# A decoder trunk on one core: the norm update's squares, gates and adds divided anew among ScalarE, VectorE and GpSimd

## The chip, the core and the metric

The kernel runs on one core of a Trainium2 chip. The metric is the device time of one execution in microseconds; the time of a kernel is the median of several executions. Five engines work side by side and meet through semaphores: TensorE (PE) multiplies matrices into PSUM, VectorE (DVE), ScalarE (ACT) and GpSimd (POOL) work elementwise, and SyncE (SP) issues most of the DMAs.

## The reference

One inference step of a trunk of four layers, D = 1024, on a prompt of 512 tokens and 8 sample sequences of one token each. Layers 0 and 3 mix tokens with a short convolution ("sconv"), layer 1 with RWKV-7, layer 2 with gated linear attention ("gla"); each is followed by a convolutional FFN ("up", "down"). Every half layer has the same frame:

```python
def rmsnorm(x, g, eps=RMS_EPS):
    xf = x.astype(jnp.float32)
    y = xf * lax.rsqrt(jnp.mean(xf * xf, axis=-1, keepdims=True) + eps)
    return (y * g.astype(jnp.float32)).astype(x.dtype)

# in trunk(), for each layer l; mod comes from the conditioning vector c
u = rmsnorm(h, norm_g[l, 0]) * (1 + sc_m) + sh_m
out = mixer(u)
h = h + gt_m * rmsnorm(out, norm_g[l, 1])
u = rmsnorm(h, norm_g[l, 2]) * (1 + sc_f) + sh_f
out = conv_ffn(u)
h = h + gt_f * rmsnorm(out, norm_g[l, 3])
```

The change is about `h = h + gate * rmsnorm(out)` and the norm of h behind it. There are eight such updates. The first follows the "out" stage of layer 0, the second the "down" stage of layer 0 (the rwkv layer comes next), and so on to the eighth, which follows "down" of layer 3 and leads to the output.

## The kernel before

All activations are held transposed: 128 channels on the partitions, tokens along the free dimension, so that h is 8 tiles of 128x520 (512 prompt tokens and 8 sample tokens) in SBUF. Weights come in blocks of 128 output channels. SyncE loads a block into one of two w_raw slots (line 523); ScalarE rounds it to w_hi (line 1037, `high`); GpSimd subtracts to get w_lo (line 814, `low`, or in four pieces in line 821, `low_parts`); TensorE runs x_hi w_hi, x_lo w_hi and x_hi w_lo (lines 1722 and 1730). SyncE may load a slot anew once the w_lo of the block in it is made. Its DMAs are issued in the order of the program, each behind its own wait, so one that waits holds all behind it.

A `plan` lists the stages in order: "pre" (the norm ahead of a half layer), the mixer's stages, "out" (output projection), "post" (the update), "pre", "up", "down", "post". Every engine walks through the plan and emits its part; nothing is reordered.

In "out" and "down" a tile of 128 output channels ends in two PSUM banks. ScalarE copies it to the SBUF slab `proj` (lines 1106 and 1107). VectorE squares it (line 3202) and adds the square to csb (lines 3217, 3225); the last tile's square is made by ScalarE straight from PSUM (`square_last`, lines 1100 and 1101).

In "post", TensorE sums the squares over the channels with ones (line 1784), ScalarE takes the root (line 1063), VectorE the reciprocal (line 2641), and TensorE spreads it over the partitions into PSUM (lines 1826 and 1828). Then, tile by tile, VectorE multiplies `proj` by it (line 2695) and does h = h + gate x proj with the gate as a scalar per partition (line 2751). Line 2739 to 2743 do the same for the sample columns. In the "pre" behind it ScalarE squares every new tile of h (line 1072) and TensorE sums it (line 1784), with two buffers between them; root, reciprocal and spreading follow once more; VectorE multiplies h by the result (line 2695), ScalarE applies scale and shift twice (lines 1137 and 1139, or 1128 and 1130 ahead of rwkv), and VectorE makes the low part. With the first tile of that the next weight matmuls begin.

Each half layer's modulation is made ahead of time by small matmuls of the conditioning vector with ada_w (line 1683). For the halves 2 to 7 part of them stands in the norm stages: 8 columns' worth in "post", and in the sums of "pre" one group behind each of the fourth to seventh sum. For those, SyncE loads six buffers (`ada_ahead`, line 547) anew after their first use (`load_again`). In the rwkv layer's first stage ("rproj"), SyncE's order is: the first weights, the rank weights w_raw from a1 and w1, the last rank weight g1, which waits for the w_lo of the block before it, and then `load_again`. GpSimd there multiplies the rank weights by a factor (line 865) and makes their low parts (line 875).

At the end TensorE transposes h back: first the sample columns of all eight tiles (line 2570), which are ready before any prompt tile and are released by the first count of h_ready, then tile by tile (line 2579); ScalarE and VectorE copy the result to y_rows, and SyncE stores it.

## Time and profile before

| | |
|---|---|
| Time, median of 3 executions | 2992.96 us (2991.05 to 2993.82) |
| The profiled execution | 2992.34 us, of which the span from first to last instruction 2990.5 us |
| Busy: PE, weight load, DVE, ACT, POOL | 95%, 91%, 51%, 36%, 44% of the span |
| Mean granted TensorE clock | 0.975 of full speed |
| DMA | 332.59 MB, 111 GB/s in the mean |

Durations in this document come from that one profiled execution. A row of the timeline has the start in us from the span's start, the time in us, the engine, the line, the operation, output<-inputs, how many instructions were merged (xN), and in brackets the idle time ahead of it and what ended it. "PEld" is TensorE's weight load, "SPq" SyncE issuing a DMA. A matmul in fp32 appears as two records. TensorE runs at 2.4 GHz or, where the throttle grants half, at 1.2 GHz.

### The profile page before, as it was taken

To read this page: it belongs to the slowest core of one execution; us is meant where nothing else is said; L and a number is where in the kernel's file an instruction comes from. 1 tells how busy PE (TensorE), PEld (TensorE's weight loads), DVE (VectorE), ACT (ScalarE), POOL (GpSimd) and SP (SyncE) were. 2 spreads that over 40 slices of the span, in tenths; PEclk is the share of its full clock that TensorE was granted. 3 is DMA by queue.
4 is the path that set the end of the run, shared out by engine and by line. 5 is a ranking of instruction groups with operands and counts; after the bars stand their busy time and mean duration, and the time that the engine had idled before them with its cause. 6 is when DMAs were issued, how large, how long until landed. Compare 5 with 4: busy or idle time off the path is not lost. (4 is left out here: it accounts for less than half of the span.)

```text
span 2990.5 us, 71312 instructions
## 1 busy us (share of the span) xinstructions
PE 2845.7 (95%) x29353; PEld 2711.8 (91%) x29353; DVE 1535.0 (51%) x2080; ACT 1062.6 (36%) x2047; POOL 1314.5 (44%) x957
## 2 busy tenths in 40 slices
PE   6999999998998999899999899999999999899998
PEld 5998999997988986899998799889999899799998
DVE  3445766117446885676603342476650444577612
ACT  3224333225455652433323543343332422433322
POOL 3443544442434563354443273434444344355443
PEclk8999999998999999999999999999999999899999
DMA  7544333444411004333344323533334543233332
GB/s 268 166 149 171 92 91 91 157 128 135 121 51 31 4 12 136 123 91 91 104 157 154 112 64 113 171 120 91 91 116 149 172 125 86 64 91 91 90 93 86
DMA packets 462286, 332.59 MB, mean 111 GB/s; under 512 B 16567, under 2 KB 432261, under 8 KB 461791
## 3 DMA queue, kind: packets, MB, share of 16 engines
q1 hardware_dynamic: 460148, 325.80, 35.2%
q10 hardware_dynamic: 1930, 3.68, 0.5%
q8 instruction: 172, 2.82, 0.4%
q14 instruction: 36, 0.29, 0.0%
HBM read 319.66 MB, written 10.20 MB: 110 GB/s over the span
## 5 line engine op out<-in xcount | busy, mean ns | idle before, releaser
L814 POOL TENSOR_TENSOR w_lo<-w_raw,w_hi 128x1024 fp32r<-128x1024 f32 x394 | 1005.0, 2551 | 1095.3 <-ACT w_hi L1037 1074.7
L1722 PE MATMUL banks<-u_hi,w_hi 128*128 128x260 f32 x4016 | 812.6, 283 | 18.9 <-ACT w_hi L1037 18.9
L1722 PE MATMUL banks<-u_lo,w_hi 128*128 128x260 f32 x4016 | 812.1, 283 | 0.0
L1722 PEld LDWEIGHTS banks<-u_hi,w_hi 128*128 128x128 f32 x4016 | 620.5, 189 | 29.4 <-issue 24.3
L1722 PEld LDWEIGHTS banks<-u_lo,w_hi 128*128 128x128 f32 x4016 | 621.6, 189 | 0.0
L1037 ACT ACTIVATE w_hi<-w_raw 128x1024 fp32r<-128x1024 f32 x402 | 424.6, 1057 | 463.9 <-PE banks L1730 296.7
L1730 PE MATMUL banks<-u_hi,w_lo 128*128 128x260 f32 x4016 | 520.7, 282 | 0.0
L1730 PEld LDWEIGHTS banks<-u_hi,w_lo 128*128 128x128 f32 x4016 | 497.0, 188 | 0.0
L1722 PE MATMUL banks<-hid_hi,w_hi 128*128 128x260 f32 x1664 | 336.4, 283 | 0.5 <-DVE hid_lo L2683 0.5
L1722 PE MATMUL banks<-hid_lo,w_hi 128*128 128x260 f32 x1664 | 335.1, 283 | 0.0
L3202 DVE TENSOR_TENSOR csb<-proj 128x520 f32 (+1 forms) x42 | 30.2, 719 | 470.2 <-ACT proj L1107 470.2
L2683 DVE TENSOR_TENSOR hid_lo<-prod,hid_hi 128x520 f32 x104 | 262.0, 2520 | 12.8
L1722 PEld LDWEIGHTS banks<-hid_hi,w_hi 128*128 128x128 f32 x1664 | 256.7, 188 | 5.7 <-issue 3.7
L1722 PEld LDWEIGHTS banks<-hid_lo,w_hi 128*128 128x128 f32 x1664 | 256.1, 188 | 0.0
L2667 DVE SCALAR_TENSOR_TENSOR conv<-gate,vecs,conv 128x536 f32<-128x536 f32 x104 | 246.9, 2374 | 15.1 <-DVE conv L2665 0.8
L1730 PE MATMUL banks<-hid_hi,w_lo 128*128 128x260 f32 x1664 | 217.0, 282 | 0.0
L1730 PEld LDWEIGHTS banks<-hid_hi,w_lo 128*128 128x128 f32 x1664 | 206.4, 188 | 0.0
L832 POOL TENSOR_TENSOR tails<-gate,ones 128x2 f32 (+1 forms) x104 | 29.2, 281 | 328.9 <-ACT gate L1595 328.9
L1602 ACT ACTIVATE conv<-conv,vecs 128x536 f32<-128x536 f32 x88 | 65.5, 744 | 288.2 <-DVE conv L2667 288.2
L1593 ACT ACTIVATE gate<-banks 128x260 f32<-128x260 f32 x88 | 34.1, 387 | 356.4 <-PE banks L1730 355.7
L2664 DVE TENSOR_SCALAR conv<-gate,vecs 128x536 f32<-128x536 f32 x104 | 57.9, 556 | 177.0 <-ACT gate L1595 173.0
L2665 DVE SCALAR_TENSOR_TENSOR conv<-gate,vecs,conv 128x536 f32<-128x536 f32 x104 | 113.8, 1095 | 15.2 <-DVE conv L2664 1.6
(471 smaller groups left out, 3840.0 us busy)
## 6 DMA issues: line engine op xcount, KB each, us to landing
w_raw<-in_ffn_w_up_dram SPq DMA_DIRECT2D x176, 512.0 KB, 3.7
ada_raw<-in_ada_w_dram SPq DMA_DIRECT2D x96, 512.0 KB, 4.7
w_raw<-in_ffn_w_down_dram SPq DMA_DIRECT2D x64, 448.0 KB, 3.7
w_raw<-in_sconv_w_in_dram SPq DMA_DIRECT2D x48, 512.0 KB, 5.0
ada_ahead<-in_ada_w_dram SPq DMA_DIRECT2D x36, 512.0 KB, 7.2
ada_ahead_down<-in_ada_w_dram SPq DMA_DIRECT2D x36, 512.0 KB, 5.9
w_raw<-in_ffn_w_down_dram SPq DMA_DIRECT2D x32, 512.0 KB, 4.0
ada_pro<-in_ada_w_dram SPq DMA_DIRECT2D x6, 2048.0 KB, 21.5
```

The lines of the kernel that those rows point to most:

```text
L814: pool.tensor_tensor(w_lo[:, s, :, :], w_raw[:, s, :, :], w_hi[:, s, :, :].bitcast(F32), ALU.subtract).then_inc(lo_done, 1)
L832: pool.tensor_tensor(to[:, 0:2], gate[:, e, TP:TP + 2], ones[:, 0:2], ALU.mult).then_inc(pool_step, 1)
L1037: act.activation(w_hi[:, s, :, :], w_raw[:, s, :, :], ACT.Copy).then_inc(hi_done, 1)
L1593: act.activation(gate[:, e, 2:2 + HALF], tile_ps[0][0][:, 0:HALF], ACT.Copy)
L1602: act.activation(conv[:, e, 0:CWD], conv[:, e, 0:CWD], ACT.Silu, bias=vec("ffn_conv_b", l * FT + m)).then_inc(silu_done, 1)
L1722: pe.matmul(tile_ps[slot][half][:, 0:HALF], w_hi[:, s, k, :], x[:, k0 + k, half * HALF:(half + 1) * HALF], start=start and k == 0 and i == ...
L1730: mm = pe.matmul(tile_ps[slot][half][:, 0:HALF], w_lo[:, s, k, :], xh[:, k0 + k, half * HALF:(half + 1) * HALF], start=False, stop=stop an ...
L2664: link(dve.tensor_scalar(conv[:, e, 0:CWD], gate[:, e, 0:CWD], w[0], None, ALU.mult))
L2665: link(dve.scalar_tensor_tensor(conv[:, e, 0:CWD], gate[:, e, 1:1 + CWD], w[1], conv[:, e, 0:CWD], ALU.mult, ALU.add))
L2667: dve.scalar_tensor_tensor(conv[:, e, 0:CWD], gate[:, e, 2:2 + CWD], w[2], conv[:, e, 0:CWD], ALU.mult, ALU.add).then_inc(conv_done, 1)
L2683: dve.tensor_tensor(lo, prod[:, e, :], hi.bitcast(F32), ALU.subtract).then_inc(hid_ready, 1)
L3202: return dve.tensor_tensor(csb[:, 1, :], o, o, ALU.mult)
```

## The change

In "out" and "down" ScalarE squares every tile straight from PSUM (`square_tile`): tile 0 into csb's first half, every other tile into the second, and VectorE only adds. The copy out of PSUM becomes `evacuate_gated`: three instructions, of which the two for the prompt tokens apply the gate as the activation's scale. In "post" VectorE multiplies two tiles at a time by the spread root and then adds tiles 3 to 7 to h; GpSimd adds tiles 0 to 2. There are two semaphores in place of one (`early_ready` for tiles 0 to 2, `h_ready` for 3 to 7), and GpSimd, ahead of its next w_lo, waits until all adds of the update are done. ScalarE's loops over "out" are written out. Some semaphores of the states of layers 1 and 2 are merged to make room for the new ones; the counts that are waited for stand for the same events.

```diff
+EARLY = 3
+LATE = KT - EARLY
+SUMMED = KT - 2
...
+                if p["kind"] == "post":
+                    for k in range(EARLY):
+                        pool.wait_ge(scaled_pair, KT // 2 * p["post"] + k // 2 + 1)
+                        pool.tensor_tensor(h[:, k, 0:TP], h[:, k, 0:TP], p["proj"][:, k, 0:TP], ALU.add)\
+                            .then_inc(early_ready, 1)
+                    if n0 < NBLK:
+                        pool.wait_ge(h_ready, LATE * (p["post"] + 2))
...
-                    act.wait_ge(h_ready, hs + k + 1)
+                    if k < EARLY:
+                        act.wait_ge(early_ready, EARLY * hs + k + 1)
+                    else:
+                        act.wait_ge(h_ready, LATE * hs + k - EARLY + 1)
...
-            def square_last(s, n, index):
-
-                act.wait_ge(sum_ready, index + 1)
+            def square_tile(s, n, index, m):
+
+                dst = csb[:, min(m, 1), :]
+                if m >= 2:
+                    act.wait_ge(sum_ready, SUMMED * index + m - 1)
                 act.wait_ge(block_done, n + 3)
-                act.activation(csb[:, 1, 0:HALF], tile_ps[s][0][:, 0:HALF], ACT.Square)
-                act.activation(csb[:, 1, HALF:T], tile_ps[s][1][:, 0:HALF], ACT.Square).then_inc(last_squared, 1)
+                act.activation(dst[:, 0:HALF], tile_ps[s][0][:, 0:HALF], ACT.Square)
+                act.activation(dst[:, HALF:T], tile_ps[s][1][:, 0:HALF], ACT.Square).then_inc(tile_squared, 1)
+
+            def evacuate_gated(s, n, mod, m, dst):
+
+                gain = mod[:, 2 * KT + m, 0:1]
+                act.wait_ge(block_done, n + 3)
+                act.activation(dst[:, TP:T], tile_ps[s][1][:, TP - HALF:HALF], ACT.Copy)
+                act.activation(dst[:, 0:HALF], tile_ps[s][0][:, 0:HALF], ACT.Copy, scale=gain)
+                return act.activation(dst[:, HALF:TP], tile_ps[s][1][:, 0:TP - HALF], ACT.Copy, scale=gain)
...
-            h_first = KT * 2 * depth
-            pe.wait_ge(h_ready, h_first + 1)
+            posts = 2 * depth
+            pe.wait_ge(h_ready, LATE * posts + 1)
             for k in range(KT):
                 mm = pe.transpose(bank[Y_RIGHT[k // 4]][0:NS, (k % 4) * P:(k % 4 + 1) * P], h[:, k, TP:T], ident[:, :])
             mm.then_inc(y_turned, 1)
             for k in range(KT):
-                pe.wait_ge(h_ready, h_first + k + 1)
+                if k < EARLY:
+                    pe.wait_ge(early_ready, EARLY * posts + k + 1)
+                else:
+                    pe.wait_ge(h_ready, LATE * posts + k - EARLY + 1)
...
-                    for k in range(KT + 1):
-                        if k < KT:
-                            step[0] += 1
-                            times_rstd(proj_x[:, k, :], proj_x[:, k, :]).then_inc(dve_step, 1)
-                        if k:
-                            dve.wait_ge(dve_step, base[0] + step[0] - (k < KT))
-                            dve.scalar_tensor_tensor(h[:, k - 1, 0:TP], proj_x[:, k - 1, 0:TP],
-                                                     mod[:, 2 * KT + k - 1, 0:1], h[:, k - 1, 0:TP], ALU.mult,
-                                                     ALU.add).then_inc(h_ready, 1)
+                    pairs = KT // 2
+                    for k in range(0, KT, 2):
+                        two = proj_x[:, k:k + 2, 0:TP]
+                        dve.tensor_tensor(two, two, rstd_ps[0].unsqueeze(1).to_broadcast([P, 2, TP]), ALU.mult)\
+                           .then_inc(scaled_pair, 1)
+                    for k in range(EARLY, KT):
+                        dve.wait_ge(scaled_pair, pairs * p["post"] + k // 2 + 1)
+                        dve.tensor_tensor(h[:, k, 0:TP], h[:, k, 0:TP], proj_x[:, k, 0:TP], ALU.add).then_inc(h_ready, 1)
...
+                    def add_square(m):
+
+                        dve.wait_ge(tile_squared, KT * index + m + 1)
+                        if m > 1:
+                            dve.wait_ge(sum_ready, SUMMED * index + m - 1)
+                        dve.tensor_tensor(csb[:, 0, :], csb[:, 0, :], csb[:, 1, :], ALU.add).then_inc(sum_ready, 1)
```

The order of instructions on GpSimd at the second update, between the "down" stage of layer 0 and the rank weights of the rwkv layer (L865 and its successor L876 scale them); before:

```order
L814 TENSOR_TENSOR w_lo<-w_raw,w_hi 128x1024 [waits hi_done]
L1010 REGISTER_ALU
L1010 COMPARE_AND_BRANCH
L821 TENSOR_TENSOR w_lo<-w_raw,w_hi 128x256 [waits hi_done]
L821 TENSOR_TENSOR w_lo<-w_raw,w_hi 128x256 x3
L865 TENSOR_TENSOR w_raw<-w_raw,vecs 128x8x64 [waits w_loaded0]
L865 TENSOR_TENSOR w_raw<-w_raw,vecs 128x8x64
L865 TENSOR_TENSOR w_raw<-w_raw,vecs 128x1024 [waits w_loaded1]
```

And the same place on GpSimd in the changed kernel:

```order
L818 TENSOR_TENSOR w_lo<-w_raw,w_hi 128x1024 [waits hi_done]
L1021 REGISTER_ALU
L1021 COMPARE_AND_BRANCH
L846 TENSOR_TENSOR h<-h,proj 128x512 [waits scaled_pair] x3
L825 TENSOR_TENSOR w_lo<-w_raw,w_hi 128x256 [waits hi_done,h_ready]
L825 TENSOR_TENSOR w_lo<-w_raw,w_hi 128x256 x3
L876 TENSOR_TENSOR w_raw<-w_raw,vecs 128x8x64 [waits w_loaded0]
L876 TENSOR_TENSOR w_raw<-w_raw,vecs 128x8x64
L876 TENSOR_TENSOR w_raw<-w_raw,vecs 128x1024 [waits w_loaded1]
```

The three adds and the wait on h_ready stand ahead of the w_lo pieces now. SyncE's order at the same place, in the changed kernel (L527 loads a weight block, L551 a buffer of modulation columns); before it has the same rows as L523 and L547:

```order
L527 DMA w_raw<-in_rwkv_w_dram 128x8x64 [waits lo_done,pack_loaded]
L527 DMA w_raw<-in_rwkv_g_dram 128x8x128 [waits lo_done]
L551 DMA ada_ahead_down_190<-in_ada_w_dram 128x1024 [waits ada_used]
L551 DMA ada_ahead_down_191<-in_ada_w_dram 128x1024 [waits ada_used]
L551 DMA ada_ahead_down_192<-in_ada_w_dram 128x1024 [waits ada_used]
```

Nothing moved on SyncE; the load of the rwkv_g weights waits on lo_done, which the w_lo pieces count. The order on TensorE at the output, in the changed kernel (L2587 turns the sample columns, L2599 the tiles):

```order
L2587 MATMUL banks<-ident,h 8x128 [waits h_ready]
L2587 MATMUL banks<-ident,h 8x128 x7
L2599 MATMUL banks<-ident,h 128x128 [waits early_ready]
L2599 MATMUL banks<-ident,h 128x128 x3
L2599 MATMUL banks<-ident,h 128x128 [waits early_ready]
```

Before, all of these wait on h_ready, whose first count stood for tile 0; now its first count of an update stands for tile 3.

## Rows read from the trace of the kernel before

**Rows 1.** Groups by line, ScalarE: busy us, mean ns | idle before us, what ended it

```profile
L1106 ACT ACTIVATE proj<-banks 128x260 f32<-128x260 f32 (+1 forms) x48 | 18.6, 388 | 170.5 <-PE banks L1730 170.5
```

**Rows 2.** Timeline, first update: start us, us, engine, line, operation [idle before <-releaser]

```profile
260.73 1.29 DVE L2695 TENSOR_TENSOR proj<-proj,banks 128x512 f32<-128x512 f32 x2 [0.19 <-PE banks L1828]
...
264.45 0.74 DVE L2751 SCALAR_TENSOR_TENSOR h<-proj,mod_m,h 128x512 f32<-128x512 f32 x1
...
265.92 0.68 PE L1784 MATMUL banks<-csb,ones 128*32 128x136 f32 x8 [0.82 <-ACT csb L1072]
...
267.53 0.68 PE L1784 MATMUL banks<-csb,ones 128*32 128x136 f32 x8
...
269.49 1.41 DVE L2751 SCALAR_TENSOR_TENSOR h<-proj,mod_m,h 128x512 f32<-128x512 f32 x2
...
272.63 0.41 PE L1784 MATMUL banks<-csb,ones 128*32 128x136 f32 x8
```

**Rows 3.** Timeline, third update

```profile
1218.77 1.28 DVE L2695 TENSOR_TENSOR proj_b<-proj_b,banks 128x512 f32<-128x512 f32 x2 [0.19 <-PE banks L1828]
...
1229.00 0.44 PE L1784 MATMUL banks<-csb,ones 128*32 128x136 f32 x8
...
1229.69 0.41 PE L1784 MATMUL banks<-csb,ones 128*32 128x136 f32 x8
```

**Rows 4.** Groups by line, nearest to the new ones; the last: ns min/median/max, first, last start

```profile
L2673 DVE TENSOR_TENSOR prod<-conv,banks 128x260 f32<-128x260 f32 x104 | 44.2, 425 | 89.8 <-ACT conv L1602 79.6 <-PE banks L1730 10.0
...
L2695 DVE TENSOR_TENSOR proj<-proj,banks 128x512 f32<-128x512 f32 x48 | 32.1, 678 | 3.0 <-PE banks L1828 2.9
...
L1595 ACT ACTIVATE gate<-banks 128x8 f32<-128x8 f32 x88 | 16.5, 187 | 0.0
...
L926 POOL TENSOR_TENSOR g_in<-g_in,g_o 128x512 f32<-128x512 f32 x8 | 10.2, 1298 | 3.1 <-ACT g_o L1396 3.1
...
L3225 DVE TENSOR_TENSOR csb<-csb x42: 699/700/2785, 217.6 to 2939.4; 128x520 f32<-128x520 f32 x42
```

**Rows 5.** GpSimd's pieces in the first update; VectorE's small add in all (ns min/median/max)

```profile
259.05 2.79 POOL L821 TENSOR_TENSOR w_lo<-w_raw,w_hi 128x256 fp32r<-128x256 f32 x4 [4.04 <-ACT w_hi L1037]
...
L2743 DVE TENSOR_TENSOR h<-h,s x8: 224/614/745, 259.9 to 2973.0; 128x64 f32<-128x64 f32 x8
```

**Rows 6.** Timeline, second update, and how long the six L547 loads took to land

```profile
671.91 2.77 POOL L821 TENSOR_TENSOR w_lo<-w_raw,w_hi 128x256 fp32r<-128x256 f32 x4
...
674.51 1.28 DVE L2695 TENSOR_TENSOR proj<-proj,banks 128x512 f32<-128x512 f32 x2 [0.43 <-PE banks L1828]
...
675.04 0.58 SPq L523 DMA_DIRECT2D w_raw<-in_rwkv_g_dram  x1
...
675.67 3.50 SPq L547 DMA_DIRECT2D ada_ahead_down<-in_ada_w_dram  x6
...
681.60 0.61 PE L1683 MATMUL banks<-ada_ahead_down,cT 128*32 128x256 f32 x8
...
687.57 0.68 PE L1784 MATMUL banks<-csb,ones 128*32 128x136 f32 x8
...
DMA to landing us min/median/max: 5.5/7.1/9.0
```

**Rows 7.** Timeline, seventh update

```profile
2579.20 1.34 PE L1784 MATMUL banks<-csb,ones 128*32 128x136 f32 x16 [0.58 <-ACT csb L1072]
```

**Rows 8.** Timeline, last update and the transposes of the output

```profile
2974.75 1.29 DVE L2695 TENSOR_TENSOR proj<-proj,banks 128x512 f32<-128x512 f32 x2 [1.50 <-PE banks L1828]
...
2976.76 1.87 PE L2570 MATMUL banks<-ident,h 128*8 128x128 f32 x8 [2.11 <-DVE h L2751]
...
2978.42 3.62 PE L2579 MATMUL banks<-ident,h 128*128 128x128 f32 x16
...
2982.66 1.07 PE L2579 MATMUL banks<-ident,h 128*128 128x128 f32 x8 [0.63 <-ACT y_rows L1641]
...
2984.32 1.32 PE L2579 MATMUL banks<-ident,h 128*128 128x128 f32 x8 [0.58 <-DVE h L2751]
```

More of the change, by code:

```diff
@@ L1114, in _ @@
                     if i:
-                        statistics(i, KT * p["post"], p["half"])
+                        statistics(i, p["post"], p["half"])
                         if p["full"]:
@@ L2613, in _ @@
             dve.wait_ge(x_copied, X0 + KT)
-            for k in range(KT):
-                dve.sem_inc(h_ready, 1)
+            dve.sem_inc(early_ready, EARLY)
+            dve.sem_inc(h_ready, LATE)
             def modulation(l, half, mod):
```

96 lines of the change are left out of this document (38 added, 58 removed).

## The prediction

> **What bounds the kernel now.** I read the page first: TensorE is busy nearly throughout, so time is won or lost only where TensorE stands still or works at its lower clock. The waits, taken by engine, say where the change's own code touches that. In the "out" and "down" stages ScalarE is the one that waits: 170.5 us ahead of 48 copies out of PSUM, 3.6 us each, always for TensorE [rows 1]. Work moved between VectorE and ScalarE there stands beside matmuls. What is left are the eight norm updates, one behind every "out" and "down", where the weight matmuls stop. I read them in the timeline, one by one.
>
> In the first one [rows 2] VectorE's first product with the root starts at 260.73, then product and gated add alternate, a tile every 1.26 us; the third tile of h is started at 264.45 and the last two end at 270.90, 10.2 us after the first product. ScalarE squares each tile and TensorE sums it. TensorE's third sum starts at 265.92, its fourth at 267.53, and from there it does not stop: between the sums it runs the next modulation's columns, 1.3 us a tile, and the eighth sum starts at 272.63, so that it ends 1.0 us later than the last square would allow (270.90, 0.7 for the square and 0.4 for the sum make 272.0; it is 273.0). So here TensorE bounds the end, not VectorE. In those microseconds TensorE is at 1.2 GHz: its 8-matmul sum takes 0.68 us where others take 0.41. In the third update the clock falls later and comes back sooner, and the eighth sum ends 11.3 us after the first product, against 12.3 in the first update [rows 2, 3]; 11.3 is what VectorE's own chain allows. Six of the eight updates have those columns between the sums, two (the last layer's) have not.
>
> **The change part by part.**
>
> *Squares and gates on ScalarE in "out" and "down".* Per tile two squares (0.39 us, as the copies of that shape [rows 1]) and one short copy (0.19 us) [rows 4] come in; VectorE loses a square and keeps the add. 56 of 64 tiles lie beside matmuls and are covered by the 3.6 us that ScalarE waits [rows 1]: nothing. If that cover were gone it would be 56 x 0.97 = 54 us; what is queued behind is the next block's w_hi copy, then GpSimd's w_lo, and both are ready microseconds before their block. At the last tile of a stage the short copy stands ahead of the root: between 0 and its 0.19 us, and the scale operand may add as much; I take 0.1 per update and count it in what follows.
>
> *Products on two tiles.* 128x512 takes 678 ns, 128x260 425 ns [rows 4]: 1.0 ns for an element and 0.16 fixed. A pair is 1.19 us; four follow each other in 4.6 us. Bounds: two old products each (1.29 x 4 = 5.2) and 4 x 1.07.
>
> *Three adds on GpSimd.* A 128x512 add of it takes 1.30 us [rows 4]. The first product pair ends at 1.2, so tiles 0, 1, 2 of h come at 2.5, 3.8 and 5.1 us after the first product. Before, the third came at 264.45 + 0.74 - 260.73 = 4.5. The third tile is 0.6 us later, 0.7 with the short copy.
>
> *Five adds on VectorE.* 0.70 us each [rows 4], start to start 0.62. Products end at 4.6, but VectorE's small add of two SBUF operands took 0.22 us at best and 0.61 in the middle of eight, in updates in which GpSimd's w_lo pieces run beside it [rows 5]; so the first add waits for GpSimd's third, to 5.1. The eighth tile is then there at 5.1 + 0.7 + 4 x 0.62 = 8.3, against 10.2: 1.8 us earlier with the 0.1.
> The Trainium skill (SBUF — State Buffer, Who interferes with whom) states the same as an exclusive lock between the two engines, and its page Perfetto Trace Analysis (Optimizing Scalar/DVE Operations) warns that offloading between these two might not help. Taken for all three adds, that is a rival below. The row beside it: two products, whose second operand is in PSUM, took 1.29 us together while GpSimd was in its four w_lo pieces [rows 2, 5], so products don't wait.
>
> *Five updates with columns between the sums (first, third to sixth).* The gain of 1.8 us at the last tile is of no use where TensorE is the bound, and TensorE's busy stretch starts with the third sum, which is 0.7 later. By the clock of each: from the third sum TensorE needs 1.6 us to the fourth and then 1.3 a tile at the lower clock, 0.7 at the higher (1229.00 to 1229.69 [rows 3]). With the lower clock up to 11.4 us after the first product, as in rows 2, three of the four tiles fall in it, and the end comes at 12.7, 0.4 later than before; where it was low for a shorter time, 0.1 to 0.2. I take 5 x 0.25 = +1.2. If the clock never fell, each would end at 0.1 + 5.1 + 0.7 + 4.1 = 10.0 instead of 11.3 to 12.3; if it stayed low throughout, 13.0: the third sum at 5.9 and the 7.1 us from 265.92 to 273.0. I keep -6 to +5.
>
> *The second update, ahead of rwkv.* Here GpSimd's w_lo pieces are put behind all adds of the update. Before, they ran at 671.91 to 674.68; SyncE, which takes its queue in order, issued the last rank weights at 675.04 after them and, behind those, six loads of modulation columns from 675.67. The first landed 5.5 us later, at 681.2, and TensorE took it at 681.60, just behind its fourth sum; the others land after 5.5 to 9.0 us [rows 6]. Now the first product starts at 674.6 instead of 674.51 and the adds end at 674.6 + 8.3 = 682.9, the pieces 2.8 later at 685.8, and the first column load is issued at 686.8. It lands at 692.3, the fourth at about 696.0. TensorE, which has the columns in line between its sums, stands from 682 to 692, then goes with the loads: the fourth's columns 0.85, the eighth sum 0.68, end at 697.5. Before, the eighth sum began at 687.57 and ended at 688.25 [rows 6]: +9.2. From below: all land in 5.5 us and the clock is high, end 695.5, +7.2; from above the fourth takes 9.0, +10.8. The scaling of the rank weights on GpSimd, that slowed the old adds, falls into this wait and costs nothing more. In the other updates the column loads stand ahead of the waiting weight load, so nothing of that.
>
> *The seventh update (no columns).* TensorE waits for ScalarE at every sum, with 0.58 us of idle time [rows 7]. The 1.8 us arrive nearly whole: -1.7 (-2.3 to -1.0).
>
> *The last update and the output.* TensorE's first transposes, of the sample columns, wait on the first h_ready, which was tile 0 and is now tile 3. Before: 1.87 us of transposes from 2976.76, then those of tiles 0 to 3 up to 2982.0 at the lower clock, a wait for ScalarE's copies, tiles 4 and 5, and the last from 2984.32 to 2985.64 [rows 8]. Now tile 3 comes at 2974.85 + 5.8 = 2980.65; 1.65 us of sample columns, 3.3 us for tiles 0 to 3, ends 2985.6; the restart lies 0.6 us behind, as before (2982.66), at 2986.3; sixteen transposes at 0.11 to 0.16 us end at 2988.0 to 2988.8. +2.5 (+1.5 to +4.0); what follows is unchanged.
>
> The sum: +1.2 + 9.2 - 1.7 + 2.5 = +11.2 us. The profiled execution took 2992.34 us (span 2990.5), 0.6 below the median of 2992.96. 2992.34 + 11.2 = 3003.5, on the scale of the median 3004.
>
> **The rivals.**
> *The rwkv stall is hidden (A).* If TensorE's columns did not wait for these loads, or they landed in time, the second update would cost the 0.7 of its third tile and up to 1.5 us more, about half of four pieces' 2.8 us [rows 5], from GpSimd's later work holding up VectorE's sample operands: +1.2 + 1.5 - 1.7 + 2.5 = +3.5, 2996.5. For it: nothing but that the old slack between landing and use was positive, 0.4 us. Against it: the loads cannot be issued before the one ahead of them in their queue.
> *Faster (B): VectorE's chain is the bound after all.* The place is the sums of the five updates: if the longer quiet before the third sum does not hold the clock down, each ends at 10.0, -1.3 to -2.3, together -8; the seventh -1.7, the last -1.8 if its first wait were harmless, and the second -2.5, because its adds no longer meet GpSimd's scaling: -14, 2979. It decides the sign once the rwkv wait is below some 5 us. For it: the clock came back within 3 us in the third update. Against it: the order of SyncE's queue and the first transposes' wait, both plain in the code.
> *The port (C).* If products also gave way to GpSimd, adds and products would alternate: the third tile at 8.6 instead of 5.1, the eighth at 11.8. From the last add's 3.5 us follow +3.2 for each of five, +12.7 for the second, +1.6, +6: +36, 3029. Against it the products' 1.29 us in rows 2.
>
> **How the numbers follow.** Forecast 0.76, A 0.14, B 0.05, C 0.05. The forecast's own range adds the bounds, not all at one end: 2998 to 3010. A is partly below it, so the range is 2996 to 3011. A change under 0.2%, 6 us, can't be told from none: 2987 to 2999. Slower takes C and all but 0.04 of the forecast, 0.77; no change takes that 0.04 and all but 0.01 of A, 0.17; faster B and the rest of A, 0.06.
>
> **What would show it.** A wait of some 10 us of TensorE before the fifth sum of the second update, released by a DMA of ada_ahead_down, and column loads issued about 11 us later than 675.67; pair products of 1.19 us and GpSimd adds near 1.3; the first VectorE add ending with GpSimd's third plus 0.7; in the first update an eighth sum that ends 11.3 to 13 us after the first product; in the seventh a root 1.7 us earlier; at the end TensorE idle until 5.8 us after the first product. I am wrong if the second update is not the largest difference, or if an "out" or "down" stage is longer by over 1 us, which would mean that ScalarE's cover was not there.

## The result, and the profile after

The changed kernel takes 3001.19 us (median of 10 runs, 2996.77 to 3003.94), the kernel before 2992.01 us (10 runs, 2987.46 to 2997.91): ratio 1.003, 95% interval 1.0022 to 1.0038. It is slower by 9 us, and the time lies 3 us from the forecast 3004. The profiled execution has a span of 3000.2 us against 2990.5, so 9.7 us to explain.

The new operations first: groups by line, the columns as in rows 1.

```profile
L1116 ACT ACTIVATE csb<-banks 128x260 f32<-128x260 f32 x64 | 24.8, 388 | 243.1 <-PE banks L1747 239.4 <-PEq L1886 3.7
...
L1124 ACT ACTIVATE proj<-banks,mod_f 128x260 f32<-128x260 f32 x32 | 15.8, 493 | 0.0
...
L2770 DVE TENSOR_TENSOR proj<-proj,banks 128x1024 f32<-128x1024 f32 x24 | 27.7, 1216 | 4.3 <-PE banks L1845 4.3
...
L846 POOL TENSOR_TENSOR h<-h,proj 128x512 f32<-128x512 f32 x18 | 22.4, 1273 | 42.6 <-DVE proj L2770 42.6
...
L2774 DVE TENSOR_TENSOR h<-h,proj 128x512 f32<-128x512 f32 x30 | 20.8, 753 | 0.0
```

ScalarE still waits 3.8 us ahead of each tile (243.1 / 64), although a tile costs it more. A pair product takes 1.22 us, a GpSimd add 1.27. The scale operand makes a copy 0.10 us longer (0.493 against the 0.388 of [rows 1]).

A useful measure of an update is the time from VectorE's first product to its next reciprocal (for the last one, to the end of the span), since the rest of the program hangs on that. In us:

| update | 1 | 2 | 3 | 4 | 5 | 6 | 7 | 8 |
|---|---|---|---|---|---|---|---|---|
| before | 12.79 | 14.21 | 11.81 | 11.97 | 11.81 | 12.67 | 12.04 | 15.75 |
| after | 13.31 | 22.05 | 11.95 | 11.88 | 11.96 | 11.90 | 10.45 | 17.58 |
| forecast, change | +0.25 | +9.2 | +0.25 | +0.25 | +0.25 | +0.25 | -1.7 | +2.5 |
| measured, change | +0.52 | +7.84 | +0.14 | -0.09 | +0.15 | -0.77 | -1.59 | +1.83 |

The eight changes sum to +8.03 us; the other 1.7 lie in the stages between. (A stage is counted here from the reciprocal that ends one update to the first product of the next.) The second update alone has 7.8. Its timeline, for [rows 6]:

```profile
675.32 4.62 DVE L2770 TENSOR_TENSOR proj<-proj,banks 128x1024 f32<-128x1024 f32 x4 [0.58 <-PE banks L1845]
...
676.62 3.74 POOL L846 TENSOR_TENSOR h<-h,proj 128x512 f32<-128x512 f32 x3 [3.96 <-DVE proj L2770]
...
679.86 3.46 DVE L2774 TENSOR_TENSOR h<-h,proj 128x512 f32<-128x512 f32 x5
...
683.40 2.77 POOL L825 TENSOR_TENSOR w_lo<-w_raw,w_hi 128x256 fp32r<-128x256 f32 x4 [3.03 <-DVE h L2774]
...
686.20 0.37 SPq L527 DMA_DIRECT2D w_raw<-in_rwkv_g_dram  x1
686.61 2.98 SPq L551 DMA_DIRECT2D ada_ahead_down<-in_ada_w_dram  x6
...
691.44 1.08 PE L1700 MATMUL banks<-ada_ahead_down,cT 128*32 128x256 f32 x8 [8.06 <-DMA ada_ahead_down<-in_ada_w_dram]
...
696.21 0.68 PE L1801 MATMUL banks<-csb,ones 128*32 128x136 f32 x8
```

Read it upward: TensorE stands 8.06 us for a DMA; SyncE issued that one at 686.61 (before: 675.67), right behind the rank weights; those waited for GpSimd's pieces, which now begin at the last add's end.

The third update, for [rows 3]: the third sum starts 5.8 us after the first product, and from there TensorE does not stop although all of h is there at 1234.45:

```profile
1229.75 0.44 PE L1801 MATMUL banks<-csb,ones 128*32 128x136 f32 x8 [1.54 <-ACT csb L1086]
...
1232.22 0.44 PE L1801 MATMUL banks<-csb,ones 128*32 128x136 f32 x8 [0.80 <-ACT csb L1086]
...
1234.46 0.68 PE L1801 MATMUL banks<-csb,ones 128*32 128x136 f32 x8
...
1237.51 0.41 PE L1801 MATMUL banks<-csb,ones 128*32 128x136 f32 x8
```

And the last, for [rows 8], where the first transposes wait for tile 3, the first that VectorE adds, 5.63 us after the first product:

```profile
2982.62 4.61 DVE L2770 TENSOR_TENSOR proj<-proj,banks 128x1024 f32<-128x1024 f32 x4 [1.33 <-PE banks L1845]
...
2988.25 1.87 PE L2587 MATMUL banks<-ident,h 128*8 128x128 f32 x8 [5.74 <-DVE h L2774]
2989.91 2.47 PE L2599 MATMUL banks<-ident,h 128*128 128x128 f32 x16
...
2993.32 1.94 PE L2599 MATMUL banks<-ident,h 128*128 128x128 f32 x16 [0.94 <-ACT y_rows L1658]
```

### The profile page after: what moved, and what is told of

Its sections match the earlier page's. It is cut to its first block and busy times, and to the rows that moved or that the text cites. A ratio compares the mean times of both kernels' runs of the same rounds, so it can differ in the third digit from the quotient of the medians.

```text
span 3000.2 us, 71163 instructions
## 1 busy us (share of the span) xinstructions
PE 2843.8 (95%) x29353; PEld 2712.5 (90%) x29353; DVE 1454.9 (48%) x1952; ACT 1107.7 (37%) x2223; POOL 1324.9 (44%) x981
## 5 line engine op out<-in xcount | busy, mean ns | idle before, releaser
L818 POOL TENSOR_TENSOR w_lo<-w_raw,w_hi 128x1024 fp32r<-128x1024 f32 x394 | 986.1, 2503 | 1096.6 <-ACT w_hi L1048 1076.1
L3221 DVE TENSOR_TENSOR csb<-csb 128x520 f32<-128x520 f32 x48 | 35.7, 743 | 570.4 <-ACT csb L1117 570.4
```

What stands on the lines that cost most here:

```text
L818: pool.tensor_tensor(w_lo[:, s, :, :], w_raw[:, s, :, :], w_hi[:, s, :, :].bitcast(F32), ALU.subtract).then_inc(lo_done, 1)
L3221: dve.tensor_tensor(csb[:, 0, :], csb[:, 0, :], csb[:, 1, :], ALU.add).then_inc(sum_ready, 1)
```

## Experiments

Each was timed against the kernel before on the same chip. Distances below are from first product to next reciprocal, as in the table.

**after_again.** No edit.

> The changed kernel once more, beside the three below. Theory (queue): 8 of its 9.7 us lie in the eight updates, 7.8 of them in the second; the stages between differ by +1.15, -0.80, -0.91, +1.44, +1.73, -0.99, +0.16 and +0.35 us, and these are the scatter of single executions. Then here the same seam figures return within 0.2 us (22.0 from the first product to the next root in the second update, 10.4 in the seventh), while the stages' differences come out with other signs, and the ratio is 1.003. Rival (ScalarE's added work lengthens the out and down stages): the same stages are longer again, by over 1 us each.

Ratio 1.0034 (1.0022 to 1.0045). The eight distances were 12.78, 22.03, 11.94, 11.88, 12.75, 11.89, 10.46, 18.40. Second and seventh return within 0.02 us; first, fifth and last do not (by 0.5 to 0.8). So the expectation of 0.2 us for all was too narrow. What differs from execution to execution is the clock: the fifth update took 11.96 us at a mean granted clock of 0.86 and 12.75 us at 0.73. The other half of the expectation missed as well: the differences between the stages and those of the kernel before kept their signs, all eight. Of the stages, only the rwkv one is far off: 525.18 us against 529.08, and 530.05 before. Over all fourteen profiles of this study that stage took 524.8 to 534.8 us whatever the edit, and it carries most of the scatter of the total; its cause stays open.
The rival's sign appeared in two places: the stages ahead of the fourth and fifth update were over 1 us longer in both profiles (396.75 us before, 398.14 and 398.14; 306.25 before, 307.97 and 307.58), the other six not in both. In the first of these it is not ScalarE's new work: counted from the first product of the third update, TensorE's 341st matmul comes 1.4 us late and its 3410th too, so all of it arises in the first 42 us, in "up", where nothing was edited. What lengthens the two stages stands below, under what was not foreseen.

**lows_first_rwkv, loads_ahead_of_g1, before_lows_late: the queue.** The first moves GpSimd's pieces, the second only SyncE's order, the third puts the wait into the kernel before.

```
 # lows_first_rwkv
+lows_first = p["kind"] == "post" and p["post"] == 1
+if lows_first:
+    low_parts(n0 + 1, 1)
 if p["kind"] == "post":
...
-    if n0 < NBLK:
+    if n0 < NBLK and not lows_first:
         pool.wait_ge(h_ready, LATE * (p["post"] + 2))
 # loads_ahead_of_g1 (the call behind the loop goes)
+if k == 3:
+    load_again(2 * l + 1)
 if k % 2:
     load_block(n0 + k, 1, A["rwkv_g1"][j].rearrange("(k p) c -> p k c", p=P))
 # before_lows_late (in the kernel before)
+if p["kind"] == "post" and p["post"] == 1:
+    pool.wait_ge(h_ready, KT * (p["post"] + 2))
 low_parts(n0 + 1, 1)
```

> The changed kernel with one thing moved: in the second update GpSimd makes its four w_lo pieces ahead of its three adds, without the wait for h, as in the kernel before. Queue theory: the column loads are issued near the first product's start again, TensorE does not stand before the fifth sum, and the distance from first product to next root falls from 22.0 to 12 to 13.5 us; the time is 7.5 to 9.5 us under the changed kernel's, within 0.1% of the kernel before. Rival (the stall has another cause, a busy DMA system or TensorE's clock): at most 2 us of it goes.

> The changed kernel with GpSimd's order left as it is; in SyncE's queue the six column loads and the pair behind them stand ahead of the last rank-weight load instead of behind it. Queue theory: the loads no longer wait for GpSimd's pieces, so the distance from first product to next root is 12 to 14 us here too, and 7 to 9 us of the time go. Rival A (what costs is that GpSimd's pieces come late for the rwkv blocks themselves): then the stall moves to the first rwkv matmuls or the rank weights, and less than 3 us go. The rank-weight load itself still comes 11 us later than in the kernel before; if its block is on the path, up to 5 us stay.

> The kernel before with one wait added: in its second update GpSimd's four w_lo pieces wait for the eighth tile of h. Nothing else of the change is in it. Queue theory: the pieces start at 686.1 instead of 671.9, the column loads are issued about 3 us later than in the changed kernel (adds end at 11.6 us after the first product, not 8.0), and the second update is 10 to 13 us longer, ratio 1.0035 to 1.0045. Rival (the stall needs the changed kernel's ScalarE or GpSimd work as well): under 5 us, ratio under 1.0015.

| kernel | 2nd update, us | ratio to before |
|---|---|---|
| changed | 22.0 | 1.0034 (1.0022 to 1.0045) |
| lows_first_rwkv | 13.09 | 1.0011 (1.0000 to 1.0021) |
| loads_ahead_of_g1 | 12.93 | 1.0018 (1.0009 to 1.0028) |
| before_lows_late | 23.47 | 1.0038 (1.0024 to 1.0051) |

The stall goes with either cure, and one wait in the kernel before brings it back whole, +9.26 us in that update (10 to 13 were expected; the pieces started at 684.33, not at 686.1). Its timeline, with the same chain as above:

```profile
684.33 2.76 POOL L821 TENSOR_TENSOR w_lo<-w_raw,w_hi 128x256 fp32r<-128x256 f32 x4 [12.91 <-DVE h L2753]
...
687.53 3.11 SPq L547 DMA_DIRECT2D ada_ahead_down<-in_ada_w_dram  x6
...
692.39 1.08 PE L1685 MATMUL banks<-ada_ahead_down,cT 128*32 128x256 f32 x8 [10.82 <-DMA ada_ahead_down<-in_ada_w_dram]
```

The two cures differ in what they leave. With SyncE's order changed the loads are early, the rank weights still late; the timeline shows the bill behind the update:

```profile
676.30 3.97 SPq L551 DMA_DIRECT2D ada_ahead_down<-in_ada_w_dram  x6
...
686.62 0.38 SPq L527 DMA_DIRECT2D w_raw<-in_rwkv_g_dram  x1
...
695.38 1.06 ACT L1145 ACTIVATE dw_hi<-w_raw 128x1024 fp32r<-128x1024 f32 x1 [5.63 <-POOL w_raw L877]
...
697.29 0.65 PE L1763 MATMUL banks<-xb_hi,w_hi 128*128 128x260 f32 x2 [3.73 <-ACT xb_hi L1153]
```

ScalarE waits 5.63 us for the scaled weights, and its activations queue behind. The first rwkv matmul comes 8.6 us after the reciprocal, against 6.6 in the changed kernel (697.37 to 703.99) and 6.7 with the pieces first (688.29 to 694.99). So part of the stall moved on, 2 us, as its rival A had half said, and of the 7 to 9 us that were expected to go, 1.0034 less 1.0018 is 5. With the pieces first, GpSimd's scaling meets VectorE's adds instead, five adds in 6.86 us instead of 3.46:

```profile
679.73 6.86 DVE L2777 TENSOR_TENSOR h<-h,proj 128x512 f32<-128x512 f32 x5
680.19 5.25 POOL L879 TENSOR_TENSOR w_raw<-w_raw,vecs 128x512 f32<-128x512 f32 x3
```

With the pieces first the time fell by 0.23%, 7 us, where 7.5 to 9.5 were expected, and 1.0011 is the edge of the expected 0.1% above before.

**lows_first_final_early: the last update.** The pieces first, and:

```
-pe.wait_ge(h_ready, LATE * posts + 1)
+pe.wait_ge(early_ready, EARLY * posts + 1)
```

> Two things mended in the changed kernel: GpSimd's w_lo pieces ahead of its adds in the second update (as before), and TensorE's first transposes at the end wait for the first tile of h that GpSimd adds, instead of the fourth tile. If that wait is the last update's loss, the sample transposes start 2.5 us after the first product instead of 5.6, the sixteen of the last four tiles end near 10 us instead of 12.6, and from first product to the end it is 14.5 us instead of 17.4; the ratio to the kernel before is 0.9995 to 1.0005. Rival (the end is set by the copies and the output's DMAs, or by the clock): it stays at 16.5 us or more, and the ratio at 1.001.

```profile
2975.02 4.61 DVE L2773 TENSOR_TENSOR proj<-proj,banks 128x1024 f32<-128x1024 f32 x4 [1.39 <-PE banks L1848]
...
2977.64 1.87 PE L2590 MATMUL banks<-ident,h 128*8 128x128 f32 x8 [2.74 <-POOL h L849]
2979.31 3.62 PE L2602 MATMUL banks<-ident,h 128*128 128x128 f32 x16
...
2983.55 1.94 PE L2602 MATMUL banks<-ident,h 128*128 128x128 f32 x16 [0.63 <-ACT y_rows L1661]
```

The wait was the loss: 15.38 us instead of 17.41, 0.4 under before. It missed 14.5 because the sixteen transposes of tiles 0 to 3 took 3.62 us at 1.2 GHz (granted clock 0.50), not 2.47 as in the changed kernel's first profile, where the clock rose while they ran (0.77). Ratio 1.0003 (0.9992 to 1.0013).

**adds_all_vector, four_adds_gpsimd, scalar_part_alone: the parts of the change.**

```
 # adds_all_vector: GpSimd's loop goes; on VectorE, behind the four products
-for k in range(EARLY, KT):
+for k in range(KT):
     dve.wait_ge(scaled_pair, pairs * p["post"] + k // 2 + 1)
...
 # four_adds_gpsimd
-EARLY = 3
+EARLY = 4
 # scalar_part_alone: GpSimd's adds and its wait go; on VectorE
+for k in range(KT + 1):
+    if k < KT:
+        dve.tensor_tensor(proj_x[:, k, 0:TP], proj_x[:, k, 0:TP], rstd_ps[0], ALU.mult)
...
+    if k:
+        dve.tensor_tensor(h[:, k - 1, 0:TP], h[:, k - 1, 0:TP], proj_x[:, k - 1, 0:TP], ALU.add)
...
```

> The changed kernel with its three GpSimd adds given back to VectorE, behind the four products. Theory (TensorE is the bound from the third sum, and the third tile sets it): the third tile comes at 6.5 us after the first product instead of 5.1 and the eighth at 9.7 instead of 8.0, so the updates with columns are 1.3 to 1.5 us longer each, the second 1.7, the seventh 1.7, the last 1.3: about 11 us over the changed kernel, ratio to before 1.006 to 1.007. The first add on VectorE takes 0.68 us, since nothing holds the port. Rival (the columns hide it, TensorE has slack): under 4 us, ratio under 1.0045.

> The changed kernel with four adds on GpSimd instead of three. Theory (VectorE's add of two SBUF operands waits until GpSimd's adds are done): GpSimd's fourth ends at 6.3 us after the first product, VectorE's first add starts at 4.6 as before but lasts 2.2 to 2.4 us instead of 1.06, and the eighth tile comes at 8.6 to 8.8 us, 0.7 later than with three, though VectorE has one add less. Rival (they only slow each other, or share by turns): the first add lasts 0.7 to 1.1 us and the eighth tile comes at 7.2 to 7.6. The last update is 1 us longer, since its first transposes wait for tile 4. Ratio 1.003 to 1.004.

> Of the change only ScalarE's part: squares from PSUM and the gate with the copy. Products of one tile, adds of one tile on VectorE in alternation, GpSimd's pieces where they were. By the prediction it costs nothing: the out and down stages as long as before within the clock's scatter, the distances from first product to next root within 0.3 us of before, or up to 0.4 shorter since the add takes 0.68 instead of 0.74 us; ratio 0.9993 to 1.0005. Rival (ScalarE's 54 us more show): out and down stages longer by 1 us each, ratio over 1.002.

*adds_all_vector*: ratio 1.0079 (1.0066 to 1.0093); updates 3 to 6 took 14.77, 14.73, 13.93 and 14.99 us, 2.0 to 3.1 more than with GpSimd's help, more than the 1.3 to 1.5 expected. The eighth tile came 9.4 us after the product, but the third sum 1.5 us later than in the changed kernel (1235.98 - 1228.65 = 7.3, against 5.8), and more of what follows it fell into the low clock: the granted clock of the third update is 0.77 against 0.86, and the sums take 0.68 us up to the seventh.

```profile
1235.98 0.68 PE L1797 MATMUL banks<-csb,ones 128*32 128x136 f32 x8 [0.25 <-ACT csb L1082]
...
1241.52 0.68 PE L1797 MATMUL banks<-csb,ones 128*32 128x136 f32 x8
...
1242.53 0.40 PE L1797 MATMUL banks<-csb,ones 128*32 128x136 f32 x8
```

*four_adds_gpsimd*: ratio 1.0059 (1.0045 to 1.0073), 0.002 above what was expected; updates 3, 4 and 6 took 13.8 us, since tile 3 now comes 6.7 us after the first product (1234.12 - 1227.41), not 5.6, and TensorE's full stretch starts behind it; the clock had a part in it, 0.75 against 0.86 in the third update. The eighth tile came 8.46 us after the first product (theory 8.6 to 8.8, rival 7.2 to 7.6), so the sum of the theory held, but not its manner. The last update, expected 1 us longer, took 17.72 against 17.58 and 18.40. Narrow windows of the timeline show VectorE's adds of tiles 4 and 5 and GpSimd's of tile 3:

```profile
1231.94 1.05 DVE L2774 TENSOR_TENSOR h<-h,proj_b 128x512 f32<-128x512 f32 x1
...
1232.39 1.73 POOL L846 TENSOR_TENSOR h<-h,proj_b 128x512 f32<-128x512 f32 x1
...
1232.92 1.75 DVE L2774 TENSOR_TENSOR h<-h,proj_b 128x512 f32<-128x512 f32 x1
```

They take turns, instruction by instruction. VectorE's first ends at 1232.99, 0.55 after GpSimd's third (1231.16 + 1.28 = 1232.44); GpSimd's fourth, caught behind it, lasts 1.73 instead of 1.27 and ends at 1234.12; VectorE's second ends 0.55 after that, at 1234.67. In the changed kernel there is one such meeting: GpSimd's third ends at 1231.50, VectorE's first at 1232.04. The pair products beside GpSimd's adds kept their 1.21 us in both.

*scalar_part_alone*: ratio 1.0005 (0.9996 to 1.0014). Updates 3, 4, 6 and 7 took 11.39, 11.44, 11.62 and 11.56 us, all shorter than before, and by more than the 0.4 us that were expected; a product and a plain add take 1.20 us a tile instead of 1.26. The fifth took 12.51, 0.7 longer, at a granted clock of 0.73 instead of 0.86. The last took 18.31, since the late release of the transposes was left in. The part cost nothing that the clock's scatter would not hide.

**filled_idle, third_tile_early, third_early_filled, filled_to_measure: what bounds TensorE.** The granted clock was 1.2 GHz for some microseconds after TensorE's idle time in nearly every update. The filled kernels put useless matmuls in that time; third_tile_early leaves GpSimd tiles 1 and 5 only. The excerpts below leave out how the readers of h wait for the new order of adds in third_tile_early and, in the filled kernels, one wait of TensorE for the PSUM bank that the idle matmuls write.

```
 # on top of lows_first_final_early
+def warm(n):
+    for _ in range(n):
+        pe.matmul(bank[0][:, 0:P], ident[:, :], ident[:, :], start=True, stop=True)
 for k in range(KT):
+    if in_norms(half) and k < 3:
+        warm(5 if k else 9)
     pe.wait_ge(sq_done, KT * i + k + 1)
 # filled_to_measure: 5, 3, 3, and in the seventh update 10, 2, 2 and 5 ahead of the root's spread
-        warm(5 if k else 9)
+        warm(3 if k else 5)
+    elif i and k < 3:
+        warm(2 if k else 10)
 # third_tile_early, on VectorE behind each pair product (GpSimd: for k in (1, 5))
+    for m in (k, k + 1):
+        if m in POOLED:
+            continue
+        dve.wait_ge(scaled_pair, pairs * p["post"] + k // 2 + 1)
+        dve.tensor_tensor(h[:, m, 0:TP], h[:, m, 0:TP], proj_x[:, m, 0:TP], ALU.add)
```

> The kernel with both mends (pieces first in the second update, early transposes at the end), and on TensorE 9, 5 and 5 idle matmuls of 128x128 whose result nobody uses, ahead of the first, second and third sum of the six updates with columns. They fill the 1.5, 0.8 and 0.8 us in which TensorE waits there. Theory (the 1.2 GHz spell after that idle time is what makes TensorE the bound): the granted clock stays at 2.4 GHz or falls later and shorter, the eighth sum follows the eighth square, and from first product to next root it is 10.0 to 10.8 us instead of 11.9 to 13.0: 1.2 to 2 us in each of five, 6 to 9 in all, ratio 0.9970 to 0.9985. Rival (the clock falls for another reason than idle time, or the columns' own work sets the end at either clock): within 0.4 us of 11.9, ratio 1.0000 to 1.0010.

> The kernel with both mends, and another order of the adds: VectorE adds tiles 0, 2, 3, 4, 6 and 7, each right behind its pair product, GpSimd only tiles 1 and 5, each from the end of the add of the tile before. Tiles come at about 1.9, 3.2, 3.8, 4.4, 6.2, 7.5, 8.1 and 8.7 us after the first product instead of 2.5, 3.8, 5.1, 5.6, 6.2, 6.8, 7.4, 8.0: the third 1.3 earlier, the eighth 0.7 later. Theory (in the updates with columns the third sum starts TensorE's full stretch): from first product to next root 10.6 to 11.0 us instead of 11.9 in each of five, the seventh 0.5 longer than now; 4.5 to 6.5 us less, ratio 0.9980 to 0.9990. Rival (the eighth tile bounds): each 0.7 us longer, ratio 1.001 to 1.002.

> Both of the two above in one kernel. If idle time sets the clock and the third tile the start, the eighth tile (8.7 us) becomes the bound: from first product to next root 10.3 to 10.6 us in the updates with columns, so no better than the filled kernel with the old order (10.0 to 10.8); ratio 0.9970 to 0.9980. If filling does nothing to the clock, as the kernel with the new order alone, or up to 0.5 us worse in each, since the idle matmuls then stand in the way of the earlier sums.

> As the filled kernel (both mends, the old order of adds), but with as many idle matmuls as the gaps hold: in the run before each 128x128 idle matmul took 0.127 us a pass, two passes each, so that 9, 5 and 5 made 2.3, 1.4 and 1.4 us and pushed the third sum from 5.8 to 7.3 us after the first product. Now 5, 3 and 3 in the updates with columns (1.3, 0.76, 0.76 us); and in the seventh, which has no columns and was at 1.2 GHz throughout, 5 ahead of the spread of the root, 10 ahead of the first sum, 2 ahead of the second and third. Theory (TensorE at 2.4 GHz from the third sum on): third sum at 5.8, then 0.93 and four times 0.67, end 9.8, next root at 10.2 to 10.4 us after the first product instead of 11.76; five or six times 1.4 us less, and the seventh 0.3 to 0.6 shorter plus 0.9 in the spread behind it. Ratio to before 0.9945 to 0.9965. Rival (the smaller filling lets the clock fall again, since TensorE still stands 0.1 to 0.3 us at a time): 11.9 to 13 us as without filling, ratio 0.9995 to 1.0010.

| kernel | updates 1, 3, 4, 5, 6, us | 7th | ratio to before |
|---|---|---|---|
| lows_first_final_early | 12.93, 11.83, 11.95, 13.04, 11.88 | 10.46 | 1.0003 (0.9992 to 1.0013) |
| filled_idle | 11.75, 11.76, 11.76, 11.76, 11.76 | 10.46 | 0.9982 (0.9973 to 0.9991) |
| third_tile_early | 12.53, 10.63, 12.24, 11.14, 11.27 | 11.03 | 0.9988 (0.9979 to 0.9997) |
| third_early_filled | 11.76, 11.76, 11.75, 11.75, 11.75 | 11.03 | 0.9991 (0.9981 to 1.0001) |
| filled_to_measure | 10.28, 10.29, 10.27, 10.28, 10.28 | 9.75 | 0.9956 (0.9939 to 0.9972) |

Busy time by windows, one row for each kernel, from the first product to the next reciprocal of the third update (start:end, length; busy us of PE, PEld, DVE, ACT and POOL; then granted clock, DMA share, GB/s). The kernel before:

```profile
1218.77:1230.58 11.81, 8.40 (x132) 4.17 (x124) 10.17 (x17) 5.74 (x10) 1.11 (x2) 0.86 1.03 386
```

The changed kernel, and with it, in the last row, its seventh update:

```profile
1226.45:1238.40 11.95, 8.33 (x132) 4.66 (x124) 8.00 (x10) 5.66 (x10) 6.54 (x7) 0.86 0.95 363
...
2578.32:2588.77 10.45, 5.05 (x64) 1.61 (x64) 7.99 (x9) 5.21 (x9) 6.12 (x7) 0.50 0.00 0
```

Filled with 9, 5 and 5:

```profile
1213.22:1224.98 11.76, 11.28 (x170) 8.26 (x162) 8.02 (x9) 5.75 (x10) 6.57 (x7) 1.00 0.96 348
```

Filled with 5, 3 and 3, and its seventh update:

```profile
1217.79:1228.08 10.29, 9.58 (x154) 6.46 (x146) 8.02 (x10) 5.66 (x10) 5.96 (x7) 1.00 0.96 351
...
2558.41:2568.16 9.75, 6.92 (x92) 4.24 (x90) 8.00 (x10) 5.21 (x9) 5.41 (x6) 1.00 0.00 0
```

With the idle time filled the clock stayed at 2.4 GHz (1.00) in all these updates, and the scatter between them is gone. The second update is not in the table: filled with 9, 5 and 5 it took 13.78 us, with 5, 3 and 3 13.10, as long as the 13.10 of lows_first_final_early, though it was at 1.00 too. The first filling missed its 10.0 to 10.8 because the idle matmuls took 2.3, 1.4 and 1.4 us, more than the gaps hold; its last ones stood ahead of the third sum, as the timeline shows for the third update, first with 9, 5 and 5:

```profile
1219.17 1.38 PE L1834 MATMUL banks<-ident 128*128 128x128 f32 x10
1220.48 0.44 PE L1804 MATMUL banks<-csb,ones 128*32 128x136 f32 x8
```

7.3 us after the first product (1213.22), and then with 5, 3 and 3, 5.8 us after it (1217.79):

```profile
1222.71 0.94 PE L1834 MATMUL banks<-ident 128*128 128x128 f32 x6
1223.58 0.44 PE L1804 MATMUL banks<-csb,ones 128*32 128x136 f32 x8
```

From there 0.93 and four times 0.67 us, 10.28 in all: the sum made before the run (10.2 to 10.4). third_tile_early reached its 10.6 only where the clock happened to hold (third update, 1.00 throughout); elsewhere it was up to 1.9 us longer, at a granted clock of 0.85 to 0.72. With 9, 5 and 5 idle matmuls ahead it missed its 10.3 to 10.6 and gained nothing, because they, not the tiles, set the third sum.

filled_to_measure, 2979.49 us against 2993.75 on the same chip, beats both kernels: 0.44% under before (0.28 to 0.61). What the change itself is worth in that is not shown: no run put idle matmuls into the kernel before. An estimate: there VectorE's chain allows an end 11.3 us after the first product [rows 3], and the reciprocal came 0.5 us behind that end (11.81), so each of the five updates would be about 1.5 us longer than 10.28.

## Why the prediction was right

The forecast of +11.2 us was a sum of four terms. In the updates +8.03 us was measured, 3.2 less, and each term is taken up below. The spans of the two profiles differ by 9.7 us because the stages between added 1.7, which no term had: so much of the closeness is luck.

*ScalarE, nothing.* Right: the waits of 3.8 us are still there, scalar_part_alone is at 1.0005, and the stage ahead of the fourth update took 396.75 us before and 396.79 to 396.84 in the four kernels with ScalarE's part that had the same granted clock there (below). The 0.1 us per update for the short copy ahead of the root is there too: from the start of the last weight matmul to the first product of the first and of the third update it was 4.68 us, and is 4.75 in the changed kernel. Open is a rest: by the medians each kernel's difference from the kernel before is between 1 us less and 5.5 us more than the changes of its updates add up to in one profile, but before_lows_late, without ScalarE's part, has 3.4 more too.

*Products and adds.* 1.22 us a pair (1.19 forecast), 1.27 a GpSimd add (1.30), four products in 4.6 (4.6), eighth tile at 8.0 (8.3). VectorE's first add did end with GpSimd's third plus a rest, 0.54 and not 0.70. That it waits for the one instruction of GpSimd in progress and not for all of them, four_adds_gpsimd showed; with three adds the two readings give the same number.
The Trainium skill's exclusive lock (SBUF — State Buffer, Who interferes with whom) agrees with these rows for two SBUF operands as to who waits. The Trainium skill also warns that offloading between the two engines might not help (Perfetto Trace Analysis, Optimizing Scalar/DVE Operations). Here it did help: without GpSimd's three adds the kernel is 0.45% slower still (1.0079 against 1.0034). A fourth add on GpSimd cost 0.25% (1.0059). The three stand beside VectorE's products, whose second operand is in PSUM and which took 1.21 us all the same.

*Five updates with columns, +1.2.* Measured -0.05, and +0.19 in the second profile; the sign of each was luck. The mechanism was right: the third sum, at 5.8 us, starts a full stretch of TensorE, and the 1.8 us gained at the last tile are lost there (11.95 us with the eighth tile at 8.0). The size held where the clock did the same before and after (0.73 and 0.74 in the first update, 0.86 in the third to fifth): +0.52, +0.14, -0.09 and +0.15, 0.18 in the mean against 0.25. The sixth went from 0.73 to 0.86, and with that came its -0.77. I took the long low-clock spells of the kernel before as a given, and they move: the changed kernel's second profile had 0.73 in the fifth update and 12.75 us. What the prediction kept as a bound, "if the clock never fell, each would end at 10.0", is filled_to_measure's 10.28.

*The second update, +9.2.* Measured +7.84. Link by link: adds ended at 8.0 and not 8.3, the load was issued 11.3 us after the first product and not 12.2, and landed in 4.8 us and not 5.5. Shown by both cures and by the wait put into the kernel before. TensorE stood 8.06 us for the first load, and not 10. This was the largest term, and rival A is excluded by the wait for the DMA.

*The seventh, -1.7:* -1.59, and -1.58 in every other kernel with this order of adds and nothing filled in there. *The last, +2.5:* +1.83 and +2.65 in two profiles; the transposes began at 5.63 us (5.8), and the clock during the next sixteen made the difference (2.47 us in the first profile, 3.62 in the second).

*Not foreseen:* the 1.7 us between the updates. By stages they are +1.09, -0.80, -0.95, +1.39, +1.72, -1.05, +0.18 and +0.11 us. The prediction named a stage that is longer by over 1 us as a sign that ScalarE's cover was not there, so the fourth and fifth need a cause. Ten-microsecond windows that start 30 us after the first product of the third update, in the next "up" stage, for before, changed kernel and before_lows_late in turn:

```profile
1248.77:1258.77 10.00, 8.97 (x75) 9.01 (x76) 8.36 (x10) 4.47 (x8) 6.86 (x6) 1.00 0.19 56
```
```profile
1256.45:1266.45 10.00, 8.82 (x63) 8.85 (x64) 8.29 (x9) 4.11 (x8) 6.12 (x6) 0.83 0.20 55
```
```profile
1255.60:1265.60 10.00, 8.96 (x52) 8.99 (x53) 7.61 (x8) 2.94 (x5) 5.41 (x3) 0.66 0.20 59
```

75, 63 and 52 matmuls in ten microseconds of full work. In some profiles the clock falls a second time behind an update, and the stage is longer by what that costs:

| kernel | ScalarE's part in it | granted clock in the window | stage ahead of the fourth update, us |
|---|---|---|---|
| before | no | 1.00 | 396.75 |
| scalar_part_alone | yes | 1.00 | 396.82 |
| lows_first_final_early | yes | 1.00 | 396.82 |
| filled_idle | yes | 1.00 | 396.79 |
| filled_to_measure | yes | 1.00 | 396.84 |
| changed, both profiles | yes | 0.83 | 398.14 |
| before_lows_late | no | 0.66 | 399.42 |

At the same clock ScalarE's part adds at most 0.1 us. Four more kernels had 0.83 in the window and 398.2 to 398.4 us; in two, loads_ahead_of_g1 (397.49) and four_adds_gpsimd (399.00), the clock was low in the first ten microseconds of the stage as well or instead. The stage ahead of the sixth update goes by the clock as well (399.4 and 399.5 us without ScalarE's part, at 0.66 in the ten microseconds from 17 us behind the reciprocal; 398.2 to 398.4 with it, at 0.83; 396.8 in two kernels with it, at 1.00). Why the clock falls this second time in one kernel and not in another that is the same up to there, no run shows.

The excess of the fifth stage has two parts. By the count of matmuls TensorE is 0.3 us early in the changed kernel up to 239 us behind the reciprocal, and 0.95 late from 259 on; there the low clock lasts longer. The windows from 245 to 260 us, before and changed:

```profile
1884.30:1899.30 15.00, 12.66 (x80) 10.86 (x81) 7.03 (x16) 5.24 (x10) 10.95 (x8) 0.77 0.13 37
```
```profile
1893.42:1908.42 15.00, 12.86 (x72) 10.95 (x73) 5.25 (x14) 6.00 (x12) 9.10 (x7) 0.66 0.12 36
```

The last 0.8 us go by the landing of one weight load of the next "up" stage. ScalarE's w_hi copy waits for it, GpSimd's w_lo for the copy, and VectorE's small product ahead of the reciprocal, with two SBUF operands, for GpSimd. First the w_hi copy in the kernel before, then the three instructions in the changed kernel:

```profile
1939.38 1.06 ACT L1037 ACTIVATE w_hi<-w_raw 128x1024 fp32r<-128x1024 f32 x1 [3.80 <-DMA w_raw<-in_ffn_w_up_dram]
```
```profile
1950.22 1.06 ACT L1048 ACTIVATE w_hi<-w_raw 128x1024 fp32r<-128x1024 f32 x1 [3.70 <-DMA w_raw<-in_ffn_w_up_dram]
1951.35 2.38 POOL L818 TENSOR_TENSOR w_lo<-w_raw,w_hi 128x1024 fp32r<-128x1024 f32 x1 [7.14 <-ACT w_hi L1048]
...
1952.73 1.09 DVE L2761 TENSOR_TENSOR s<-proj_b,mod_m 128x64 f32<-128x64 f32 x1 [6.27 <-ACT proj_b L1125]
```

From the w_hi copy's start to the first product of the fifth update it is 6.17 or 6.18 us in thirteen of the fourteen profiles (1945.55 - 1939.38, 1956.39 - 1950.22; 6.53 in four_adds_gpsimd). From the start of the last weight matmul to that product it is 5.1 to 7.1 us, as the load lands; ahead of the sixth update it is 4.7 to 4.8. Whether ScalarE's part has a share in the late landings is not shown: 5.13 and 5.14 us in two kernels with it are as short as the 5.11 and 5.23 without.

So a sign of being wrong came up, and not for the cause that it was meant to show. Effects of 1 us cannot be read from one pair of profiles. Rivals B (-14 us) and C (+36) are excluded by the sign and by the products' 1.21 us. Two readings in the prediction's case for its rivals are off without moving the forecast: the low clock of the third update lasted some 3.3 us, not under 3 (0.86 in the mean of 11.81 us), and rival A's sum leaves out the 0.7 us of the third tile that its text gives.

## What to carry to other kernels

When a step is moved behind others on an engine, follow its semaphore into the DMA queue: the cost was not the 2.8 us of GpSimd's pieces, nor their own consumer (which cost 2 us once the loads were cured), but six loads for TensorE that stood behind one waiting load in an in-order queue. Where a chain before TensorE is shortened, look at whether TensorE then runs a full stretch at the low clock; if so, the gain showed here only after the clock was held (here by matmuls that fit in the gaps) or its first input came sooner (third_tile_early). Adds split off to GpSimd paid here beside VectorE's products with a PSUM operand; the fourth, which ran against VectorE's own adds, cost time. Before an effect of 1 us is given to an edit, compare the granted clock of the same stretch in both profiles.

## What the runs showed of the hardware

- Idle matmuls in gaps of 1.5, 0.8 and 0.8 us kept TensorE at 2.4 GHz through updates in which it was otherwise at 1.2 for 3 to 7 us, and through the seventh, where it was at 1.2 from one end to the other (0.50 against 1.00). With a gap of 0.24 us left in the third update (1.18 in the seventh) the clock was still 1.00. An idle matmul of 128x128 in float32 is two passes; nine took 2.27 us, 0.25 each.
- VectorE and GpSimd, both with two SBUF operands, take turns instruction by instruction; a caught 128x512 add ends 0.54 to 0.55 us after the other engine's instruction (VectorE) or 1.13 us after (GpSimd), less than the 0.68 and 1.27 of a free one. VectorE's 128x64 product, 0.23 us when free, took 1.09 beside a w_lo of GpSimd and ended 0.08 us after it.
- A VectorE product of 128x1024 with a broadcast PSUM operand took 1.21 us beside GpSimd's adds or not (after, four_adds_gpsimd: all four products of the third update).
- The same copy out of PSUM on ScalarE, 128x260, took 0.388 us without and 0.493 us with the per-partition scale operand.
